# A decoder layer's expert mixer: two of nine token tiles take their v rows from one pass over the whole v table

## What is computed

```
def peer(n, wq, qn_w, k1, k2, u, v):          # n: tokens x 1024; u, v: 16384 x 1024
    q = rms_norm((n @ wq).reshape(blk, 8, 256), qn_w)
    s1 = einsum('thd,hnd->thn', q[..., :128], k1)       # 128 keys of each kind
    s2 = einsum('thd,hnd->thn', q[..., 128:], k2)
    v1, i1 = top_k(s1, 16); v2, i2 = top_k(s2, 16)
    cand = v1[..., :, None] + v2[..., None, :]          # 16 x 16 pairs
    cidx = i1[..., :, None] * 128 + i2[..., None, :]    # expert = row key * 128 + column key
    sc, sel = top_k(cand, 16)
    eidx = take_along_axis(cidx, sel)
    g = softmax(sc)
    act = gelu(einsum('td,thkd->thk', n, u[eidx]))
    return einsum('thk,thkd->td', g * act, v[eidx])
```

## Time and profile before

| | before |
|---|---|
| runs | 4419.03, 4423.56, 4429.66 us |
| median | 4423.56 us |
| profiled execution, span | 4435.7 us |
| mean granted TensorE clock | 0.843 |
| busy: PE, PE weight loads | 3251.9 us (73%), 1706.6 us (38%) |
| busy: DVE, ACT, POOL | 2593.4 us (58%), 1955.8 us (44%), 1472.8 us (33%) |
| moved by DMA | 1447.75 MB, mean 326 GB/s |

### The profile page before, as it was taken

How to read it: one execution, slowest core, us unless ns; L and a number is a source line. 1 busy time by engine, 2 the same in 40 slices (tenths; PEclk the granted TensorE clock), 3 DMA queues, 4 the chain that set the end, 5 groups by cost and what they waited for, 6 DMA issues and landing times. The chain is left out here.

```text
span 4435.7 us, 46775 instructions
## 1 busy us (share of the span) xinstructions
PE 3251.9 (73%) x14243; PEld 1706.6 (38%) x14243; DVE 2593.4 (58%) x6557; ACT 1955.8 (44%) x6710; POOL 1472.8 (33%) x1175
## 2 busy tenths in 40 slices
PE   6998868874999999786754687985555555555556
PEld 4677754642543346444432454651111111111111
DVE  2362334476557745584646536656766766766774
ACT  2122431145457734483532225544545545545554
POOL 4543102352322233231212112223444444444443
PEclk8998889986999999787976898987867677777769
DMA  6533244389999999796999978889999999999998
GB/s 258 198 138 129 71 154 171 115 347 356 393 384 356 378 365 387 288 358 232 402 315 383 369 277 308 348 321 383 421 404 421 420 404 415 413 403 414 415 407 334
DMA packets 313374, 1447.75 MB, mean 326 GB/s; under 512 B 42913, under 2 KB 104257, under 8 KB 164770
## 3 DMA queue, kind: packets, MB, share of 16 engines
q0 software_dynamic: 152064, 1107.36, 62.4%
q1 hardware_dynamic: 146690, 330.19, 21.0%
q10 hardware_dynamic: 14368, 7.21, 0.6%
HBM read 1377.25 MB, written 74.57 MB: 327 GB/s over the span
## 5 line engine op out<-in xcount | busy, mean ns | idle before, releaser
L2928 POOL DMA_INDIRECT uv_ring<-in_peer_uv,pick_idx x1024 | 1134.5, 1108 | 2255.1 <-PE expert_acc L3089 1929.2
L3089 PE MATMUL expert_acc<-uv_ring,diag 128*64 128x512 f32 x3968 | 1263.8, 773 | 665.6 <-ACT diag L3059 629.4
L3016 DVE SCALAR_TENSOR_TENSOR uv_ring<-uv_ring,n_pairs 128x1024 f32<-128x1024 f32 x1024 | 1246.5, 1230 | 672.9 <-DMA uv_ring<-in_peer_uv,pick_idx 639.9
L3089 PEld LDWEIGHTS expert_acc<-uv_ring,diag 128*64 128x64 f32 x3968 | 293.8, 163 | 1519.5 <-ACT diag L3059 994.2
L3046 ACT ACTIVATE gelu_cube<-dots_now 128x2 f32<-128x2 f32 x528 | 105.6, 200 | 929.7 <-DVE uv_ring L3016 854.3
L3054 ACT ACTIVATE pick_weight<-gelu_tanh,pick_share 128x1 f32<-128x1 f32 x1056 | 350.8, 379 | 17.6
L3059 ACT ACTIVATE diag<-half_pattern,pick_weight 128x64 f32<-128x64 f32 x1024 | 300.4, 340 | 16.6
L956 PE MATMUL h_acc_q<-in_w_all_q,n_all_q 128*128 128x512 f32 x640 | 286.8, 601 | 0.0
L3049 ACT ACTIVATE gelu_tanh<-gelu_cube,dots_now 128x1 f32<-128x1 f32 x1056 | 253.3, 286 | 16.2
L3051 ACT ACTIVATE pick_share<-dots_now,pick_prob 128x1 f32<-128x1 f32 x1056 | 245.4, 280 | 0.0
L953 PE MATMUL h_acc_q<-n_all_q,in_w_all_q 128*128 128x272 f32 x896 | 218.0, 399 | 10.0 <-DMA in_w_all_q<-in_w_in 10.0
(11 more groups left out here) (457 smaller groups left out, 4784.8 us busy)
## 6 DMA issues: line engine op xcount, KB each, us to landing
in_w_p<-in_w_in SPq DMA_DIRECT2D x34, 1024.0 KB, 7.2
in_w_all_q<-in_w_in SPq DMA_DIRECT2D x17, 2048.0 KB
ada_w<-in_w_ada SPq DMA_DIRECT2D x10, 2048.0 KB, 8.8
uv_ring<-in_peer_uv,pick_idx POOLq DMA_INDIRECT x1024
past_keys_q<-in_past_keys SPq DMA_DIRECT2D x16, 1024.0 KB
past_rows_q<-in_past_values SPq DMA_DIRECT2D x16, 1024.0 KB
score_pair<-scores SPq DMA_DIRECT2D x66, 128.0 KB
wq_raw_p<-in_peer_wq SPq DMA_DIRECT2D x16, 512.0 KB, 5.7
```

Source lines behind the costliest of these rows:

```text
L2928: pool.indirect_dma_start(self.rows_of(part, s), None, self.x["peer_uv"][0], bass.IndirectOffsetOnAxis(ap=self.idx[:, q % 2, s, k:k + 1], ...
L3016: ins = dve.scalar_tensor_tensor(out=row, in0=row, scalar=1.0, in1=self.n2[:, tile % 2, s if tile < LAST_TILE else 0, :], op0=ALU.mult, op ...
L3089: ins = pe.matmul(self.acc[s * 64:(s + 1) * 64, c, :], self.diag[:, part % DIAGS, s, :], rows, start=first, stop=last)
```

## The change

- Parts 128 to 255 (tiles 2 and 3, `DENSE`) gather only u rows, 4 KB each, from a table of their own, `peer_u`. Their slot is free when the dots are done (`dots_ready`), the lead is 3, and `weigh` and `sum_part` are left out for them. The dots, and each pick's row and column index, stay in SBUF (`picks_of`). The gelu is done for 16 parts at once: `inner` (VectorE, three operations and a product with the shares), `tanhs` (ScalarE), `dense_weights` (VectorE).
- In `experts_rest` a new class, `WholeTable`, makes the sum of the v rows of these 256 tokens as a matrix product with the whole table `peer_v` (16384 rows). Two `turn` steps transpose the picks on TensorE, so that a token is a column with its 128 picks on the partitions. Then, for each half of the 128 row keys, come 32 `octet` and 64 `block` steps. An octet is 8 tokens: for each, VectorE writes a 128x128 one-hot of the column keys (one compare with one per-partition scalar) and a 128x64 one-hot of the row keys times the weight (a compare and a product with two), TensorE multiplies the two, and ScalarE copies the result of the 8 into `dense_w`. A block is 128 rows of v that SP loads (512 KB, three slots, the third being HGRN's state buffer) and four matmul calls 128x128x512, which add up over all 128 blocks in four PSUM banks. The steps are spread evenly over turns 258 to 522 by the costs in `US`. At the end VectorE makes the residuals of tiles 2 and 3.
- No sixth slot, and 256 parts beside the stages.
- In `merge_phase`, `v_new` loses its own buffer: it is loaded into the buffer of the samples' keys, on SP behind the past values and behind a wait for the keys to be turned. The samples' gate, one score buffer and the transposed results likewise use buffers that are there already, and the constants `zeros` and `iota16` give way to one `iota` of 128 columns.

```diff
-        v_new = sb("v_new", [S_TOK, G, WIDTH])
+        v_new = k_rows[:].rearrange("p (g c) -> p g c", g=G)
...
-            sp.dma_start(v_new[:].rearrange("p a b -> p (a b)"), dram["h_r"][SEQ:TOK, R_V:R_V + G * WIDTH]).then_inc(consts_in, 16)
...
                 load_value(i)
+            sp.wait_ge(rows_turned, 1)
+            sp.dma_start(k_rows[:], dram["h_r"][SEQ:TOK, R_V:R_V + G * WIDTH]).then_inc(v_new_in, 16)
             beside.head("sp", 2)
...
-            pe.wait_ge(consts_in, 32)
+            pe.wait_ge(v_new_in, 16)
...
-MORE_FROM, MORE_TO = 33, 125
...
+DENSE = (2, 3)
+ROW_TILES = tuple(t for t in range(LAST_TILE + 1) if t not in DENSE)
+DENSE_LEAD = 3
+def tile_of(part):
+    return min(part // TILE_PARTS, LAST_TILE)
+def row_sums(parts):
+    return sum(tile_of(part) not in DENSE for part in range(parts))
...
+        lead = DENSE_LEAD if tile_of(part) in DENSE else LEAD
+        out.append((slot, list(had.setdefault(slot, [])), part - lead))
...
-        if before:
-            pool.wait_ge(self.part_free, before[-1] + 1)
+        if before and self.of_tile(before[-1]) in DENSE:
+            pool.wait_ge(self.dots_ready, before[-1] + 1)
+        elif before:
+            pool.wait_ge(self.part_free, row_sums(before[-1] + 1))
         for s in range(2):
-            pool.indirect_dma_start(self.rows_of(part, s), None, self.x["peer_uv"][0],
+            into, table = self.rows_of(part, s), self.x["peer_uv"][0]
+            if self.of_tile(part) in DENSE:
+                into, table = into[:, 0:D], self.x["peer_u"][0]
...
+            if q // 4 in DENSE:
+                for j in range(2):
+                    dve.tensor_copy(self.picks(q, j)[:, s, :], self.picked[:, j, :])
...
+            dot = self.picks(q, 2)[:, s, r:r + 1] if tile in DENSE else self.dots[:, i % DOTS, s:s + 1]
...
+        if tile in DENSE and r == TOPK - 1:
+            self.inner(q)
+        if q and self.of_tile(i - TOPK) in DENSE and r == 2:
+            self.dense_weights(q - 1)
...
+    def inner(self, q):
+        dve, link = self.nc.vector, self.dve_order.link
+        dots, cube = self.picks(q, 2), self.work[:]
+        dve.wait_ge(self.dots_ready, (q + 1) * TOPK)
+        link(dve.tensor_tensor(cube, dots, dots, ALU.mult))
+        link(dve.tensor_scalar(cube, cube, GELU_B, GELU_A, ALU.mult, ALU.add))
+        dve.tensor_tensor(cube, cube, dots, ALU.mult).then_inc(self.inner_ready, 1)
+        dve.wait_ge(self.prob_ready, 2 * (q + 1))
+        link(dve.tensor_tensor(dots, dots, self.prob[:, q % 2].rearrange("p k s -> p s k"), ALU.mult))
+    def dense_weights(self, q):
+        dve, dots = self.nc.vector, self.picks(q, 2)
+        dve.wait_ge(self.tanh_ready, self.dense_groups(q + 1))
+        dve.scalar_tensor_tensor(out=dots, in0=self.work[:], scalar=1.0, in1=dots, op0=ALU.add, op1=ALU.mult).then_inc(self.weights_ready, 1)
+    def tanhs(self, q):
+        act = self.nc.scalar
+        act.wait_ge(self.inner_ready, self.dense_groups(q + 1))
+        act.activation(self.work[:], self.work[:], ACT.Tanh).then_inc(self.tanh_ready, 1)
...
+            if self.of_tile(self.weighed) not in DENSE:
+                self.weigh(self.weighed)
...
+            if self.of_tile(self.summed) not in DENSE:
+                self.sum_part(self.summed)
...
+class WholeTable:
...
+    OCTET = 8
+    QUAD = 4
+    ONE_SLOTS = 4
+    V_SLOTS = 3
+    HALF = N_KEYS // 2
+    T = len(DENSE) * P
+    OCTETS = T // OCTET
+    STEPS = len(DENSE) + 2 * (OCTETS + HALF)
+    US = {"turn": 3.0, "octet": 3.2, "block": 3.44}
+    FROM, UNTIL = SEQ // 2 // P * TILE_PARTS + 2, N_PARTS - 6
...
+        costs = [self.US[self.kind(n)[0]] for n in range(self.STEPS)]
+        self.share = sum(costs) / (self.UNTIL - self.FROM)
...
+    def until(self, i):
+        due = (i + 1 - self.FROM) * self.share + 1e-6
+        return sum(end <= due for end in self.ends)
...
+    def sp(self, i):
+        for kind, b in self.due("sp", min(self.until(i) + 2, self.STEPS)):
+            if kind == "block":
+                self.load_block(b)
+    def load_block(self, b):
+        sp = self.nc.sync
+        at_least(sp, self.block_done, b - self.V_SLOTS + 1)
+        sp.dma_start(self.v_rows(b), self.ex.x["peer_v"][0, b * N_KEYS:(b + 1) * N_KEYS, :]).then_inc(self.v_in[b % self.V_SLOTS], 16)
...
+    def sp_end(self):
+        sp = self.nc.sync
+        sp.wait_ge(self.block_done, N_KEYS)
+        for n, tile in enumerate(DENSE):
+            sp.dma_start(self.x1_rows(n), self.ex.dram["x1"][tile * P:(tile + 1) * P, :]).then_inc(self.x1_in, 16)
...
+    def dve(self, i):
+        n = self.until(i)
+        for kind, k in self.due("dve", n):
+            if kind == "turn":
+                self.copy_turned(k)
+        for kind, k in self.due("ones", min(n + 1, self.STEPS)):
+            if kind == "octet":
+                self.ones(2 * k)
+                self.ones(2 * k + 1)
+        if n == self.STEPS and not self.ended:
+            self.ended = True
+            self.residuals()
...
+    def ones(self, quad):
+        dve = self.nc.vector
+        half, first = quad // (self.T // self.QUAD), quad * self.QUAD % self.T
+        iota = self.ex.const["iota"]
+        if quad == 0:
+            dve.wait_ge(self.turn_copied, len(DENSE))
+        at_least(dve, self.quad_done, quad - self.ONE_SLOTS + 1)
+        for j in range(self.QUAD):
+            into, token = self.one[:, quad % self.ONE_SLOTS, j], first + j
+            dve.tensor_scalar(into[:, 0:N_KEYS], iota[:], self.pick_column(1, token), None, ALU.is_equal)
+            ins = dve.tensor_scalar(into[:, N_KEYS:], iota[:, half * self.HALF:(half + 1) * self.HALF], self.pick_column(0, token),
+                                    self.pick_column(2, token), ALU.is_equal, ALU.mult)
+        ins.then_inc(self.ones_ready, 1)
...
+    def residuals(self):
+        dve = self.nc.vector
+        dve.wait_ge(self.block_done, N_KEYS)
...
+    def copy_octet(self, octet):
+        act = self.nc.scalar
+        half, k = divmod(octet, self.OCTETS)
+        act.wait_ge(self.quad_done, 2 * (octet + 1))
+        if half and k == 0:
+            act.wait_ge(self.block_done, self.HALF)
+        act.copy(self.w[:, :, k * self.OCTET:(k + 1) * self.OCTET],
+                 self.got[:, octet % 2, :].rearrange("p (t a) -> p a t", a=self.HALF)).then_inc(self.octet_copied, 1)
...
+    def octet(self, octet):
+        pe = self.nc.tensor
+        if octet == 0:
+            pe.wait_ge(self.turn_copied, len(DENSE))
+        at_least(pe, self.octet_copied, octet - 1)
+        for quad in (2 * octet, 2 * octet + 1):
+            pe.wait_ge(self.ones_ready, quad + 1)
+            for j in range(self.QUAD):
+                one, at = self.one[:, quad % self.ONE_SLOTS, j], (quad % 2 * self.QUAD + j) * self.HALF
+                ins = pe.matmul(self.got[:, octet % 2, at:at + self.HALF], one[:, 0:N_KEYS], one[:, N_KEYS:], start=True, stop=True)
+            ins.then_inc(self.quad_done, 1)
+    def block(self, b):
+        pe = self.nc.tensor
+        half, k = divmod(b, self.HALF)
+        if k == 0:
+            pe.wait_ge(self.octet_copied, (half + 1) * self.OCTETS)
+        pe.wait_ge(self.v_in[b % self.V_SLOTS], 16 * (b // self.V_SLOTS + 1))
+        for n in range(len(DENSE)):
+            for c in range(2):
+                ins = pe.matmul(self.acc[:, n, c, :], self.w[:, k, n * P:(n + 1) * P], self.v_rows(b)[:, c * BLOCK:(c + 1) * BLOCK],
+                                start=(b == 0), stop=(b == N_KEYS - 1))
+        ins.then_inc(self.block_done, 1)
...
+def experts_rest(nc, ph, experts, begin, spare):
+    dense = WholeTable(nc, ph, experts, spare)
...
+            dense.sp(i)
+        dense.sp_end()
...
+            dense.dve(i)
...
+            dense.pe(i)
...
-FRONT_PARTS = 257
+FRONT_PARTS = 256
...
-        phase(experts_rest, "_rest", True, later[0], FRONT_PARTS)
+        phase(experts_rest, "_rest", True, later[0], FRONT_PARTS, state[:].rearrange("p a h k -> p (a h k)"))
...
```

More of the change, by code:

```diff
@@ L2747, in ring_slots @@
     for part in range(N_PARTS):
-        more = MORE_FROM <= part <= MORE_TO
-        if part == MORE_FROM:
-            free.insert(0, PART_SLOTS)
-        elif part == MORE_TO + 1:
-            free.remove(PART_SLOTS)
         slot = free.pop(0)
         free.append(slot)
-        out.append((slot, list(had.setdefault(slot, [])), part - LEAD - (1 if more else 0)))
+        lead = DENSE_LEAD if tile_of(part) in DENSE else LEAD
+        out.append((slot, list(had.setdefault(slot, [])), part - lead))
         had[slot].append(part)
@@ L2794, in __init__ @@
         self.acc = bank("expert_acc", [P, 2, 512])
-        self.landed = [sem(f"landed{k}") for k in range(PART_SLOTS * 2 + 2)]
-        self.slots, self.more, self.fetched = ring_slots(), None, 0
+        self.landed = [sem(f"landed{k}") for k in range(PART_SLOTS * 2)]
+        self.slots, self.fetched = ring_slots(), 0
         self.scores_in = [sem("scores0_in"), sem("scores1_in")]
```

(19 more changed lines are left out.)

162 lines of the change are left out of this document (122 added, 40 removed).

## The result

The change made the kernel slower: 4467.72 us median of 4 runs (4456.91 to 4475.1) against 4423.19 (4419.03 to 4429.66), ratio 1.0096, 95% interval 1.0076 to 1.0115. In a second set of runs the ratio was 1.0083 (1.0055 to 1.0111). The forecast was 4468.

What follows compares the result with a forecast made beforehand. Expert gathers on full DMA bound the last stage, TensorE the projection, no single engine the stages between. Terms -227 + 168 + 5 + 74 + 10 + 5 + 3 + 6 = +44 on 4423.6 gave 4468 us, range 4350 to 4550.

Steps and rivals of the forecast that it cites:

- HGRN: Stage of 239 us: DMA falls from 191 to 120, -10; the closing signs say no gain in HGRN.
- attention: Stage of 290 us, bound by DMA: narrower gathers take 273 to 197, idle of 17 stays, -76.
- merge: Stage of 148 us, bound by DMA: 141 falls to 103, idle of 7 stays, -38.
- query: Stage of 275 us, bound by TensorE: without the sums 243.8 falls to 173.7, idle of 31 stays, -70.
- front: Stages from HGRN to query, 1193 us: narrower gathers and missing sums save 227 us, between -86 and -353.
- v table: Last stage: 128 blocks at 1.31 us each, all on full DMA's path, +168; low end 163 at 412 GB/s.
- one-hots: Last stage: octets of 3.35 us make VectorE the bound in 83 turns, +74 (0 if they hide, up to +122).
- end: End of last stage: VectorE's residual waits for the last block and two x1 loads, last dots behind, +10 (0 to 20).
- attention keeps its waits for keys: Attention: named as a sign that the prediction is wrong; TensorE's waits for keys were counted among the transfers that shrink.
- the prediction's own rule: Front stages: each takes its busiest resource's time afterwards plus the idle time that resource has today.
- Small things: Projection and front: no sixth slot +5, samples' v rows loaded later +3, copies of picks and batched gelu +6.
- The rival of VectorE and GpSimd in each other's way: Octet turns: gathers and one-hot compares block each other, +255 there, 4723 us; chance 0.05.

Runs made afterwards that it cites:

- after_again: The changed kernel once more, nothing edited, for a second profile and ratio: 4459.87 us against 4419.63.
- before_again: The kernel before once more, nothing edited, for a second profile: 4420.36 us.
- octets_thin: The changed kernel with the planner's octet cost raised from 3.2 to 6.88, spreading octets over more turns: 4404.42 us, ratio to before 0.9965.
- thin_x1: octets_thin with x1 of tiles 2 and 3 loaded early, into the one-hot buffer: 4399.05 us, ratio 0.9947.
- thin_end: thin_x1 with the residuals of tiles 2 and 3 made after the last part's dots: 4392.31 us, ratio 0.9937.
- before_narrow: The kernel before with only the gathers of tiles 2 and 3 cut to 4 KB of u; weighing, sums, slots and leads stay: 4282.73 us.
- wide_gathers: The changed kernel with tiles 2 and 3 gathering 8 KB u and v rows again, v halves not read: 4635.61 us.
- short_dots: The changed kernel with the second dot of each part of tiles 2 and 3 over 64 of 1024 columns: 4426.53 us.

## Why the prediction was right, point by point

Stage by stage, after_again against before_again:

| step | forecast | measured |
|---|---|---|
| HGRN | -10 | -4 |
| attention | -76 | -75 |
| merge | -38 | -15 |
| branch | -16 | -25 |
| out | -15.5 | -13 |
| norm 2 | -1 | -3 |
| query | -70 | -67 |
| **front** | **-227** | **-202** |
| projection ("sixth slot") | +5 | +4 |
| rest: v table, part 256, one-hots, end | +257 | +232 |

The forecast's +3 for the samples' v rows and +6 for the copies of picks and the batched gelu lie in the front too; with them its front is -218.

The direction, the stages and, but for merge and query, the bounds were right. That 4468 and 4467.72 agree to a microsecond is luck in part. The front gave 16 us less than the -218 and the rest cost 25 us less than forecast. In the second set of runs the median is 4460, and the two second profiles differ by 33 us, not 44.

- **The one-hots** decided the sign, and their price came from the right rows: 0.20 and 0.22 us forecast from the earlier trace rows, the same measured, an octet 8 x 0.418 = 3.34 us against 3.35, an octet turn some 6.1 against 6.15. The term was 74; octets_thin took 64 of it back. The Trainium skill ("VectorE: DVE Perf Modes", section "The TRN2 errata") has 58 cycles plus half the elements, which makes an estimate of 0.22 us a token; the trace has 0.418 and does not agree.
- **The v table**: 168 forecast, 164 measured. The low end, bytes at 412 GB/s, was the better price, since both kinds of transfer share full engines at 416.
- **The end**: +10 forecast, but nothing is left for it: 232 less 164, 64 and 5 is -1. The waits were there (8.8 us for x1, 7.5 for the last block), and thin_x1 showed that to remove the first alone doesn't shorten the stage. But thin_end, in which nothing stands behind either wait, has a rest 9 us shorter than thin_x1's, in one profile each. What the end costs, nothing or some 9 us, stays open.
- **Attention** came out right (-76, -75), but not by the bytes alone, which the working made its only cause: before_narrow has the bytes and gives 57, wide_gathers has all but the bytes and gives 1. The prediction also named as a sign of being wrong that attention keeps its waits for keys. It keeps more than half of them, 36.4 us (from 2041 to 2251) of the 60.3 of the earlier trace rows:

```profile
PE att_turned_q L1550 <- DMA k_raw_q<-qk_rows_dram: 36.4, 10, 6.5
```

- **HGRN** gave 4 us instead of 10. The bytes alone do give 10 (before_narrow); the rest of the change takes 6 of them back, and costs 9 where the rows stay wide (wide_gathers). The one term that the prediction had for such a cost, copies and gelu on VectorE, isn't it, for VectorE is no busier there (182 us against 183); the last section has a candidate. That the working comes to the 10 is luck as well: it added to VectorE's busy time (179, written as 181 in the sum) the 48 us that DMA, not VectorE, had idle. VectorE's own idle time was 239 - 179 = 60, and by the prediction's own rule HGRN gains nothing, as its last paragraph says too.
- **Merge**: the step that failed is the rule itself, that a stage keeps its idle time when its busiest resource gets shorter. DMA's busy time came out as forecast (0.79 x 133 = 105 against 103), but its idle went from 7 to 28, and with the bytes alone (before_narrow, 0.83 x 126 = 105) to 21. GpSimd's gathers waited there for the dots that free their slots (first line, from 2251 to 2384), and two windows of 10 us show how DMA then stops:

```profile
POOL uv_ring L2959 <- DVE uv_ring L3053: 64.3, 10, 10.9
...
2262.00:2272.00 10.00, 2.42 (x29) 1.39 (x27) 8.36 (x24) 0.21 (x1) 1.87 (x2) 0.50 1.02 352
2272.00:2282.00 10.00, 2.59 (x52) 2.62 (x56) 9.19 (x21) 0.21 (x1) 0.00 (x0) 0.50 0.28 93
```

In the second window VectorE is busy for 0.92 of the time, GpSimd issues no gather and DMA falls to 0.28. With 96 us of VectorE beside 105 of DMA, in part one after the other, the sum of the larger and today's idle was too short. short_dots confirms VectorE's part: of 15 us taken off VectorE about half reach the stage. The 8 us between before_narrow's merge and that of the change have no cause shown.
- **Query** came out right for a reason that was half right: TensorE's missing sums were said to give the 70, but each cause alone gives 25 to 29 and only both give 67.
- **Small things**: the sixth slot and the samples' v rows cost nothing by their own runs (+5 and +3 forecast), so the projection's 4 us have another, open cause. For the copies of picks and the batched gelu +6 was forecast; no run takes out these alone, and VectorE is busy for 713 us of the stages from HGRN to query afterwards, for 714 before. The rival of VectorE and GpSimd in each other's way falls, since the compares' starts lie as close as forecast and their lengths have a median near their least:

```profile
L3286 DVE TENSOR_SCALAR dense_onehots_rest<-iota,dense_picks x512: 266/277/539, 2823.4 to 3864.7; 128x128 f32<-128x128 f32 x171
```

## What to carry to other kernels

When work of two kinds is spread over a stage, one kind bound by one engine and the other by another, spread each by what the bottleneck of its own stretch has free, not by its own length: one constant turned a loss of 0.8% into a gain of 0.35%. To price a stage after a change, look at the second busiest resource too: in merge, where DMA came down to 105 us beside VectorE's 96, its idle time grew from 7 to 28 us, and query kept the second bound when only the first was taken away. And take the distance from start to start, not the printed length, as the price of a short instruction.
